# Two blocks of a language model on one core: the second token tile of x is loaded through ScalarE's queue, ahead of the norm rows and the first constants

## The chip, the core and the metric

The kernel runs on one core of a Trainium2 chip. The metric is the device time of one execution in microseconds (us), from the first instruction to the last. It is taken several times, and the median is compared.

## What is computed

The input x is 256 tokens by 1024 features, all in float32. Two layers of a first block and one layer of a second block are applied to it. Each layer of the first block is a feed-forward stage, a mixer (attention in layer 0, a state-space mixer in layer 1) and another feed-forward stage. The change touches only the very beginning, which feeds the first feed-forward stage:

```python
def rms_norm(x, g):
    xf = x.astype(jnp.float32)
    y = xf * lax.rsqrt(jnp.mean(xf * xf, axis=-1, keepdims=True) + EPS)
    return (y * g.astype(jnp.float32)).astype(x.dtype)

def swiglu(x, w_gate, w_up, w_down):
    return (jax.nn.silu(x @ w_gate) * (x @ w_up)) @ w_down

# first thing in the block
x = x + 0.5 * swiglu(rms_norm(x, ffn1_norm[i]), ffn1_w_gate[i], ffn1_w_up[i], ffn1_w_down[i])
```

## The kernel before, in words

**Tiling.** x lives in SBUF as two token tiles of 128 tokens (TT = 2), each 128 partitions by 1024 values, 512 KB. Weights come from HBM in units of 1 MB (128 x 2048 values) into three slots of `raw`. Each unit is split into a high part (`w_hi`, a copy in float32r made by ScalarE, ACT) and a low part (`w_lo`, the rest, made by VectorE, DVE). TensorE (PE) multiplies high by high, low by high and high by low. The activations are split the same way, into `hT_hi` and `hT_lo`. Programs of the engines are written out by hand and are joined by semaphores alone: an engine does its instructions in order and stops at the first one whose semaphore has not come.

**The order at the start**, which is all that the change is about:

- SyncE (SP) issues the loads of x (`start_sp`, L898 to L900), one DMA for each token tile, both counted on the semaphore `x_in`. Behind them on the same queue stand the first weights: the first unit in four DMAs of 256 KB (`first_unit`, L659 to L664: gate and up for k = 0 and 1, counted on `first_in`, then gate and up for k = 2 and 3, counted on `landed_0`), then two DMAs of 512 KB for each of units 1 and 2 (`load_unit`, L373). These eight weight loads need no wait, since the three slots are empty. The next unit waits for a slot.
- ACT issues two small loads (`start_act_loads`, L908 to L910): 64 KB of the first constants, which hold the identity matrix, and 8 KB of norm rows of ffn1 (16 x 128 values, in L905). Both are counted on `const1_in`. Then ACT waits for both (L1003), uses the identity once (L1004), which also loads its table, and waits for `cols`.
- PE (`start_pe`, L980 to L987) first does 10 matmuls on zeros (`keep_busy`, L978). Then it waits for `const1_in` to reach 32, that is, for identity and norm rows both, and transposes the norm rows (L985). Then it waits for `x_in` to reach 32, both token tiles, and transposes x in 16 pieces (L631). Four more matmuls on zeros follow, and then the first feed-forward stage, whose three kinds of products are L705, L712 and L718.
- DVE zeroes the operand of the matmuls on zeros (L1034), waits for the transposed norm rows and copies them to `cols` (L1037). ACT needs `cols` for its first `hT_hi` tile.
- After that ACT goes in this order (`start_act`): `hT_hi` tiles 0 and 1 (L553), wait for `first_in`, quarters 0 and 1 of the first unit's `w_hi` (L1009), `hT_hi` tiles 2 and 3, wait for `landed_0`, quarters 2 and 3, `hT_hi` tiles 4 and 5, unit 1's `w_hi` (L390), and so on. PE's first products need a quarter of `w_hi` and a tile of `hT_hi` each.

Of the kernel before, what the change touches and what calls it, by code (L numbers as in the profile page):

```python
# [24 lines left out]
P = 128  # L25
SEQ = 256
TT = SEQ // P
# [117 lines left out]
def build(nc, w, out):  # L145
    with ExitStack() as ctx:
        sems = {}

        def sem(name):
            if name not in sems:  # L150
                sems[name] = ctx.enter_context(nc.semaphore(name))
            return sems[name]
# [21 lines left out]
        def keep(name, shape, dt=F32):  # L174
            t, top[0] = at(top[0], name, shape, dt)
            return t
# [11 lines left out]
        x = keep("x", [P, TT, D])  # L188
# [707 lines left out]


        def start_sp(sp):  # L898
            for t in range(TT):
                sp.dma_start(x[:, t, :], w["x"][0, t * P:(t + 1) * P, :]).then_inc(sem("x_in"), 16)  # L900

        def load_rows(engine, names, landed):
            for name in names:
                a, n = ROWS[name]
                engine.dma_start(rows_in[a:a + n, :], w[name].rearrange("l (r c) -> (l r) c", c=P))\  # L905
                      .then_inc(sem(landed), 16)

        def start_act_loads(act):  # L908
            act.dma_start(const1[:, 0:P], w["first_constants"][:, 0:P]).then_inc(sem("const1_in"), 16)
            load_rows(act, ["ffn1_norm"], "const1_in")  # L910

        def start_pool(pool):
            pool.memset(neg_half[:, :], -0.5).then_inc(sem("neg_half"), 1)
# [87 lines left out]
        def start_act(act):  # L1001
            start_act_loads(act)
            act.wait_ge(sem("const1_in"), 32)  # L1003
            act.activation(table_use[:, :], ident[:, 0:1], ACT.Copy)  # L1004
            act.wait_ge(sem("cols"), 1)

            def first_hi(k):
                cs = slice(k * UNIT // 4, (k + 1) * UNIT // 4)
                act.activation(w_hi[:, 0, cs], raw[:, 0, cs], ACT.Copy).then_inc(sem("first_hi" if k < 3 else "hi_ready"), 1)  # L1009

            hT_hi_tiles(act, 0, ("ffn1_norm", 0), (0, 1))
            act.wait_ge(sem("first_in"), 16 * PARTS)
            first_hi(0)
            first_hi(1)
            hT_hi_tiles(act, 0, ("ffn1_norm", 0), (2, 3))
            act.wait_ge(sem("landed_0"), 16 * PARTS)
            first_hi(2)
            first_hi(3)
            hT_hi_tiles(act, 0, ("ffn1_norm", 0), (4, 5))
            split_hi(act, 1)  # L1020
            hT_hi_tiles(act, 0, ("ffn1_norm", 0), (6, 7))
            squares(act, 0)
            split_hi(act, 2)
# [1592 lines left out]
        @block.sync  # L2616
        def _(sp):
            start_sp(sp)
            ffn_sp(sp, "ffn1_0", FFN1, 0)
            attn_sp(sp)  # L2620
            ffn_sp(sp, "ffn2_0", FFN2, 0)
            ffn_sp(sp, "ffn1_1", FFN1, 1)
            ssm_sp(sp)
            ffn_sp(sp, "ffn2_1", FFN2, 1)
            second_sp(sp)
# [83 lines left out]
```

## Time and profile before

| | |
|---|---|
| median of 3 runs | 1322.38 us (1322.37 to 1322.51) |
| the profiled execution, its own time | 1323.11 us |
| its span, first instruction to last | 1321.3 us |
| PE busy | 1308.9 us, 99% of the span |
| DVE busy | 1079.3 us, 82% |
| ACT busy | 713.4 us, 54% |
| HBM read | 252.12 MB, 192 GB/s over the span |

The profiled execution took 0.73 us more than the median of the three runs. The rows below speak of that execution. "Busy" is time in which an instruction of the engine runs, "issue to landing" of a DMA ends when its semaphore is complete. SPq and ACTq are the queues on which SP and ACT issue DMAs. In the lists of DMA traffic, q1 is what SP issues and q10 what ACT issues, and a packet is one contiguous run of bytes on one of the 16 DMA engines, or the 4 bytes that count a semaphore up. A row of one token tile of x is a packet of 4 KB, a row of the identity matrix 512 bytes, a row of a first gate or up load 1 KB.

### The profile page before, as it was taken

The numbers are of one execution on the slowest core, as the hardware profiler recorded it, in microseconds if no ns is written. First come the engines' busy times: TensorE is split into PE (matmuls) and PEld (weight loads), VectorE is DVE, ScalarE is ACT, GpSimd is POOL, SyncE is SP. The second block draws the span as 40 slices with busy tenths as digits, with TensorE's granted clock in tenths as the row PEclk, the third lists the DMA queues.
The fourth block names the chain that finished last, engine by engine and source line by source line (L and its number), as shares of the span: only waits on it lengthen the run. The fifth ranks groups of instructions, "written<-read, shape, count | busy, mean of one in ns | idle before, by whom it ended". The sixth has DMA issues, their size and how long they took to land.

```text
span 1321.3 us, 20183 instructions
## 1 busy us (share of the span) xinstructions
PE 1308.9 (99%) x7751; PEld 1106.1 (84%) x7751; DVE 1079.3 (82%) x1592; ACT 713.4 (54%) x840; POOL 210.1 (16%) x193
## 2 busy tenths in 40 slices
PE   9999999999999999999999999999999999999998
PEld 7888888888888888888899988788888888888886
DVE  6977788868999789998786999769777767878587
ACT  6444455665444454444465688854444466558553
POOL 2400001102000010000000035300000011664940
PEclk9999999999999999999999999999999999999999
DMA  8655555528577754776544565475655554654541
GB/s 274 223 191 190 190 178 205 190 80 305 193 262 265 243 183 149 266 234 223 180 160 160 179 210 181 138 254 166 209 195 197 194 173 160 201 172 141 175 150 57
DMA packets 158445, 254.29 MB, mean 192 GB/s; under 512 B 8800, under 2 KB 99248, under 8 KB 156704
## 3 DMA queue, kind: packets, MB, share of 16 engines
q1 hardware_dynamic: 155136, 232.68, 52.1%
q0 software_dynamic: 2576, 18.45, 4.0%
q10 hardware_dynamic: 656, 2.11, 0.5%
q8 instruction: 52, 0.85, 0.2%
q14 instruction: 25, 0.20, 0.0%
HBM read 252.12 MB, written 1.08 MB: 192 GB/s over the span
## 4 chain that ended last, share of the span: by engine, by line
PE 96%; ACT 1%; DVE 1%; POOL 1%; issue 1%; DMA 0%; SPq 0%; POOLq 0%; DVEq 0%; ACTq 0%
PE psum L712 12%; PE psum L718 12%; PE psum L705 12%; PE psum L737 5%; PE psum L736 5%; PE psum L735 5%; PE psum L2003 4%; PE psum L2005 4%; PE psum L2004 4%; PE psum L438 2%; PE psum L439 2%; PE psum L445 2%; PE psum L473 2%; PE psum L481 2%; PE psum L475 2%; PE psum L504 2%
## 5 line engine op out<-in xcount | busy, mean ns | idle before, releaser
L390 ACT ACTIVATE w_hi<-raw 128x2048 fp32r<-128x2048 f32 (+1 forms) x220 | 419.8, 1910 | 316.4 <-PE psum L718 121.5
L402 DVE TENSOR_TENSOR w_lo<-raw,w_hi 128x2048 fp32r<-128x2048 f32 x219 | 507.3, 2337 | 100.2 <-ACT w_hi L390 98.7
L839 DVE STREAM_TRANSPOSE hidT<-hid 32x128 f32<-32x128 f32 x704 | 213.1, 303 | 22.1
L705 PE MATMUL psum<-w_hi,hT 128*128 128x512 f32 x704 | 174.6, 390 | 0.1
L718 PE MATMUL psum<-w_lo,hT 128*128 128x512 f32 x704 | 173.9, 389 | 0.0
L712 PE MATMUL psum<-w_hi,hT 128*128 128x512 f32 x704 | 173.9, 389 | 0.0
L712 PEld LDWEIGHTS psum<-w_hi,hT 128*128 128x128 f32 x704 | 132.2, 188 | 27.4
L718 PEld LDWEIGHTS psum<-w_lo,hT 128*128 128x128 f32 x704 | 132.2, 188 | 27.4
L705 PEld LDWEIGHTS psum<-w_hi,hT 128*128 128x128 f32 x704 | 131.9, 188 | 27.8 <-ACT w_hi L1009 0.8
L786 ACT ACTIVATE silu_g<-psum,rstd 128x256 f32<-128x256 f32 x88 | 36.9, 471 | 113.2 <-PE psum L718 107.6
L2003 PE MATMUL psum<-w_hi,hT 128*128 128x512 f32 x224 | 88.8, 397 | 0.0
L2005 PE MATMUL psum<-w_hi,hT 128*128 128x512 f32 x224 | 87.4, 390 | 0.0
L2004 PE MATMUL psum<-w_lo,hT 128*128 128x512 f32 x224 | 87.3, 390 | 0.0
L473 PE MATMUL psum<-hT,w_hi 128*128 128x256 f32 x256 | 62.6, 285 | 0.0
L737 PE MATMUL psum<-w_hi,odd_hidT_lo 128*128 128x512 f32 x160 | 62.3, 389 | 0.0
L735 PE MATMUL psum<-w_hi,hidT_hi 128*128 128x512 f32 x160 | 62.3, 389 | 0.0
L736 PE MATMUL psum<-w_lo,hidT_hi 128*128 128x512 f32 x160 | 62.3, 389 | 0.0
L735 PE MATMUL psum<-w_hi,odd_hidT_hi 128*128 128x512 f32 x160 | 62.3, 389 | 0.0
L737 PE MATMUL psum<-w_hi,hidT_lo 128*128 128x512 f32 x160 | 62.3, 389 | 0.0
L736 PE MATMUL psum<-w_lo,odd_hidT_hi 128*128 128x512 f32 x160 | 62.3, 389 | 0.0
L475 PE MATMUL psum<-hT,w_lo 128*128 128x256 f32 x256 | 62.1, 283 | 0.0
L830 DVE TENSOR_TENSOR hid<-psum,silu_g 128x512 f32<-128x512 f32 x44 | 30.3, 689 | 36.7 <-ACT silu_g L786 36.7
(407 smaller groups left out, 2186.1 us busy)
## 6 DMA issues: line engine op xcount, KB each, us to landing
raw<-in_ffn_w_down SPq DMA_DIRECT2D x88, 512.0 KB, 4.9
raw<-in_ffn_w_gate SPq DMA_DIRECT2D x87, 512.0 KB, 3.8
raw<-in_ffn_w_up SPq DMA_DIRECT2D x87, 512.0 KB, 5.1
raw<-in_w_in SPq DMA_DIRECT2D x72, 512.0 KB, 4.5
raw<-in_ssm_w_in SPq DMA_DIRECT2D x48, 512.0 KB, 4.6
raw<-in_attn_w_qkv SPq DMA_DIRECT2D x24, 512.0 KB, 4.6
ada_in<-in_w_ada POOLq DMA_DIRECT2D x8, 1536.0 KB, 7.2
raw<-in_ssm_w_out SPq DMA_DIRECT2D x16, 512.0 KB, 4.3
```

Source lines behind the costliest of these rows:

```text
L390: act.activation(to, src, ACT.Copy).then_inc(sem("hi_ready"), 1)
L402: dve.tensor_tensor(to, src, hi.bitcast(F32), ALU.subtract).then_inc(sem("lo_ready"), 1)
L705: pe.matmul(psum[:, banks[t], :], hT_hi[:, k, t * P:(t + 1) * P], hi[:, kk, :], start=k == 0, stop=False)
L712: pe.matmul(psum[:, banks[t], :], hT_lo[:, k, t * P:(t + 1) * P], hi[:, kk, :], start=False, stop=False)
L718: m = pe.matmul(psum[:, banks[t], :], hT_hi[:, k, t * P:(t + 1) * P], lo[:, kk, :], start=False, stop=k == KD - 1)
L735: pe.matmul(to, a, hi[:, k, cs], start=start and k == 0, stop=False)
L736: pe.matmul(to, a, lo[:, k, cs], start=False, stop=False)
L737: m = pe.matmul(to, b, hi[:, k, cs], start=False, stop=False)
L839: dve.transpose(to[:, :, :, 32 * a:32 * (a + 1)], src[:, :, :, 32 * b:32 * (b + 1)])\
L2003: pe.matmul(to, a, hi[:, kk, :], start=k == 0, stop=False)
L2004: pe.matmul(to, a, lo[:, kk, :], start=False, stop=False)
L2005: m = pe.matmul(to, b, hi[:, kk, :], start=False, stop=k == KD - 1)
```

## The change

```diff
         def start_sp(sp):
-            for t in range(TT):
-                sp.dma_start(x[:, t, :], w["x"][0, t * P:(t + 1) * P, :]).then_inc(sem("x_in"), 16)
+            sp.dma_start(x[:, 0, :], w["x"][0, 0:P, :]).then_inc(sem("x_in"), 16)
...
         def start_act_loads(act):
+            act.dma_start(x[:, 1, :], w["x"][0, P:2 * P, :]).then_inc(sem("x_in"), 16)
+            load_rows(act, ["ffn1_norm"], "const1_in")
             act.dma_start(const1[:, 0:P], w["first_constants"][:, 0:P]).then_inc(sem("const1_in"), 16)
-            load_rows(act, ["ffn1_norm"], "const1_in")
```

SP loads only the first token tile of x, and its weight loads move up by one place. ACT loads the second token tile first, then the norm rows, then the identity matrix. No wait is added or removed, and no byte more or less is loaded. Two places of the program differ, both queues of loads.

ACT's instructions at the start of the program (L908 is the load of the second token tile, L904 that of the norm rows, L910 that of the identity; L1004 is the first instruction that needs them):

```order
@@ -1,5 +1,6 @@
 L2642 UNCONDITIONAL_BRANCH
-L909 DMA const_58<-in_first_constants 128x128
-L905 DMA rows_in<-in_ffn_norm 16x128
+L908 DMA x<-in_x 128x1024
+L904 DMA rows_in<-in_ffn_norm 16x128
+L910 DMA const_58<-in_first_constants 128x128
 L1004 ACT_TABLE_LOAD
```

The identity goes from first to third place, and a load eight times its size now stands ahead of it.

SP's instructions at the start of the program (L663 issues the first unit's quarters of 256 KB):

```order
@@ -1,4 +1,4 @@
 L2616 UNCONDITIONAL_BRANCH
-L900 DMA x<-in_x 128x1024 x2
+L899 DMA x<-in_x 128x1024
 L663 DMA raw<-in_ffn_w_gate 128x2x256
 L663 DMA raw<-in_ffn_w_up 128x2x256
```

One load less stands ahead of the first weights. The instructions of PE, DVE and GpSimd are the same in both, and their order too.

## Rows read from the trace of the kernel before

**Rows 1.** The page: busy time of each engine, and the chain that ended last

```profile
PE 1308.9 (99%) x7751; PEld 1106.1 (84%) x7751; DVE 1079.3 (82%) x1592; ACT 713.4 (54%) x840; POOL 210.1 (16%) x193
...
PE 96%; ACT 1%; DVE 1%; POOL 1%; issue 1%; DMA 0%; SPq 0%; POOLq 0%; DVEq 0%; ACTq 0%
```

**Rows 2.** Chain that ended last, first 12.5 us: start, duration, what

```profile
1.65 0.43 SPq L663
...
2.12 6.19 DMA raw<-in_ffn_w_up
...
8.33 1.16 ACT w_hi L1009 x2
9.49 0.72 ACT hT L553 x2
10.21 0.53 ACT w_hi L1009
...
10.78 1.25 PE psum L705 x4
```

**Rows 3.** Timeline, first 9 us: start, duration, what, idle time before it

```profile
0.74 0.86 SPq L900 DMA_DIRECT2D x<-in_x  x2
0.74 0.41 ACTq L909 DMA_DIRECT2D const<-in_first_constants  x1
...
1.18 0.45 ACTq L905 DMA_DIRECT2D rows_in<-in_ffn_norm  x1
...
1.45 4.41 PE L978 MATMUL psum<-hidT_lo 128*128 128x512 f32 x10 [1.45 <-DVE hidT_lo L1034]
...
6.16 0.20 ACT L1004 ACTIVATE half_rstd_and_use<-const 128x1 f32<-128x1 f32 x1 [3.21 <-DMA rows_in<-in_ffn_norm]
...
6.18 0.23 PE L985 MATMUL psum<-const,rows_in 16*128 16x16 f32 x1 [0.31 <-DMA rows_in<-in_ffn_norm]
...
6.86 1.97 PE L631 MATMUL psum<-const,x 128*128 128x128 f32 x16 [0.45 <-DMA x<-in_x]
7.40 0.84 ACT L553 ACTIVATE hT<-psum,cols 128x256 fp32r<-128x256 f32 x2 [1.04 <-PE psum L631]
```

**Rows 4.** The instructions of tile x: time from issue to landing of its two loads

```profile
DMA to landing us min/median/max: 4.7/5.2/5.6
```

**Rows 5.** Stretches of half a microsecond: busy time of each engine, PEclk, DMA share, GB/s

```profile
2.50:3.00 0.50, 0.50 (x3) 0.40 (x2) 0.00 (x0) 0.44 (x1) 0.00 (x0) 1.00 0.34 90
3.00:3.50 0.50, 0.50 (x3) 0.40 (x2) 0.00 (x0) 0.00 (x0) 0.00 (x0) 1.00 0.66 116
...
4.50:5.00 0.50, 0.50 (x2) 0.34 (x2) 0.00 (x0) 0.00 (x0) 0.00 (x0) 1.00 1.07 420
6.00:6.50 0.50, 0.23 (x1) 0.13 (x1) 0.06 (x1) 0.20 (x1) 0.00 (x0) 1.00 1.07 381
```

**Rows 6.** DMA traffic from 0 to 4.0 us, by queue: packets, MB, share of 16 engines

```profile
q1 hardware_dynamic: 88, 0.36, 33.7%
q10 hardware_dynamic: 58, 0.03, 9.0%
```

**Rows 7.** DMA traffic by queue from 4.25 to 4.5 us

```profile
q1 hardware_dynamic: 28, 0.09, 88.8%
q10 hardware_dynamic: 30, 0.01, 17.6%
```

**Rows 8.** DMA traffic by queue from 4.75 to 5.0 us

```profile
q1 hardware_dynamic: 26, 0.10, 99.6%
q10 hardware_dynamic: 16, 0.00, 7.7%
```

**Rows 9.** DMA traffic by queue from 6.25 to 6.5 us

```profile
q1 hardware_dynamic: 97, 0.09, 104.2%
```

**Rows 10.** Timeline, 5 to 15 us: start, duration, what, idle time before it

```profile
6.83 1.81 SPq L373 DMA_DIRECT2D raw<-in_ffn_w_up  x1
...
9.59 2.44 PE L705 MATMUL psum<-w_hi,hT 128*128 128x512 f32 x8
...
11.30 0.30 PEld L705 LDWEIGHTS psum<-w_hi,hT 128*128 128x128 f32 x2 [0.22 <-ACT w_hi L1009]
...
12.85 1.92 ACT L390 ACTIVATE w_hi<-raw 128x2048 fp32r<-128x2048 f32 x1 [0.88 <-DMA raw<-in_ffn_w_up]
```

**Rows 11.** Chain that ended last, 12 to 40 us: start, duration, what

```profile
15.70 1.81 PE psum L705 x8
17.51 1.81 PE psum L712 x8
```

## The prediction

> **What bounds the kernel now.** I began with the page: PE is busy for 99% of the span and makes 96% of the chain that ended last; DMA is 0% of it, rounded [rows 1]. So loads can matter only where PE has nothing to do yet. The change touches just such a place. Its whole field is the start, so I went on to the chain of the first 12.5 us, from its end backwards [rows 2]. PE's products L705 at 10.78 wait for the third quarter of w_hi, which ACT ends at 10.74. That stands in ACT's order behind two hT tiles and two earlier quarters, which began at 8.33. The trace puts this start down to the load of the first up weights, issued at 2.12 and landed 6.19 later, at 8.31. But the timeline shows a second cause that was nearly as late: ACT's first two hT tiles ran from 7.40 for 0.84, to 8.24 [rows 3]. The gap is 0.09 us. So **two chains meet at 8.3**: the first weights (8.31), and x to transposes to hT (8.24). Whichever ends later starts w_hi.
>
> I then followed the second chain back [rows 3]. ACT's hT began 0.54 after PE's first transpose of x at 6.86. That transpose waited for x: the second load of x is the one issued at about 1.18 (two issues in 0.86 from 0.74), and the longer landing time of 5.6 [rows 4] puts it at 6.8. Before it PE had transposed the norm rows at 6.18, released by identity and norm rows together, so const1_in was complete at about 6.15. That leaves const1_in a **slack of some 0.6 us** ahead of x before it delays anything. The change spends this slack: it puts 512 KB ahead of what const1_in counts.
>
> Last I looked at how DMA engines share their time. Between 2.5 and 3.5 us they are busy for only 0.34 and 0.66 of the time, though all of x has been issued; from 4.5 on they are full at 380 to 420 GB/s [rows 5]. In the full phase the two queues take turns packet by packet: 28 packets of q1 go with 30 of q10 in 0.25 us [rows 7]. One packet of 4 KB takes 0.25 x 16 x 99.6% / 26 = 0.15 us of an engine, one of 512 bytes 0.25 x 16 x 7.7% / 16 = 0.02 us [rows 8], one of 1 KB 0.25 x 16 x 104.2% / 97 = 0.04 us [rows 9].
>
> **The change part by part.**
>
> *Issuing.* SP issues one load less ahead of the weights, 0.43 us; ACT one more. ACT's table load and L1004 come later by that, but ACT sat idle 3.21 us before L1004 [rows 3], which hides it. On SP the later loads gain nothing from it: the last of them took 1.81 us merely to issue [rows 10], since the queues are full and the bytes set the pace. All bytes that have to land before 8.31 (both tiles of x, constants, first gate and up) are the same as before. Cost 0, gain in the second term below.
>
> *x lands earlier.* Ahead of the last row of x, an engine used to carry 8 packets of the identity and one of norm rows, 9 x 0.02 = 0.2 us. These now come behind it. That gives 6.8 - 0.2 = 6.6. There may be more, from the half-empty start. Up to 4.0 us q10 carried 58 packets with 0.03 MB, and q1 88 with 0.36 MB [rows 6]. If q10's packets are as many when they are rows of x, they carry 58 x 4 KB = 0.24 MB, that is 0.21 MB more by 4.0, and at the 0.10 MB in 0.25 us of the full phase [rows 8] this is 0.5 us. If the start is slow because of the bytes, it is 0. No row shows which engine waits for what there, and the last engine counts, so I take the middle, 0.25, and keep 0 and 0.5 as ends. x_in is complete at about **6.35** (6.1 to 6.6).
>
> *const1_in lands later.* Behind the last row of x, an engine has one packet of norm rows and 8 of the identity, with their two counting packets. Taking turns with SP's queue, where rows of 1 KB now stand, this takes 9 to 11 x (0.02 + 0.04) = 0.6 us. If nothing took turns it would be 0.2. So const1_in is complete at 6.35 + 0.6 = **6.95** (6.55 to 7.2), 0.8 later than before, and **it, not x, is what PE waits for last**.
>
> *What hangs on it.* PE transposes the norm rows 0.03 after, and the transposes of x follow one matmul later; these are 0.11 apart (16 in 1.97 with the tail of the last [rows 3]). So the first starts at 6.95 + 0.03 + 0.11 = 7.09, against 6.86: +0.23. Queued behind it on PE are all other transposes, the four matmuls on zeros and L705. DVE's copy to cols takes its turn beside the transposes, as before. ACT's hT pair ends at 8.24 + 0.23 = 8.47. The first weights landed at 8.31 at the latest, so hT now sets the start of w_hi: 8.33 + 0.23 - 0.09 = 8.47 or so, **+0.14**, rounded +0.15. From there ACT's work is the same, and PE's waits for w_hi at 10.78 and 11.30 [rows 2, 10] move along.
>
> *Is the delay taken up later?* ACT has an idle 0.88 before unit 1's w_hi at 12.85 [rows 10], so ACT recovers. PE doesn't: after 11.3 it runs product after product, 8 in 1.81 us, with no gap [rows 11], and for the rest of the program it is the 96% of the chain. So the +0.15 stays to the end, and so would a gain. Weights are no danger: unit 1 is split at 12.85 + 1.92 = 14.77, PE comes to it at 15.70.
>
> **The sum**: 1321.3 + 0.15 = 1321.45 of span in a profiled execution whose own time would be 1323.11 + 0.15 = 1323.26; on the median of the runs shown, 1322.38 + 0.15 = **1322.5 us**. Bounds of the unknown terms: const1_in at 7.2 with no gain at the start gives 7.34 - 6.86 - 0.09 = +0.4. The start's full gain of 0.5 with a batch of small packets gives const1_in at 6.3 and transposes at 6.44, -0.42 - 0.09 = -0.5, and weights 0.5 earlier allow it. So the bounds are -0.5 and +0.4.
>
> A rule speaks against the change's first part. The packets of the two queues lie on the same 16 engines, whose share reaches 1.07 [rows 5]. The Trainium skill, "DMA: Bandwidth & Descriptors", section "Issuing engines are not separate DMA queues", says that issuing from several engines saves only the sequencer's issue time. By it the start's fill would be at most the 0.43 us of one issue, and the sum would hardly differ.
>
> **The rivals.**
>
> 1. *Coarse turns, slower.* The place is PE's wait for const1_in. If an engine carries a whole load of one queue (16 rows of 1 KB and a count, 17 x 0.04 = 0.7 us) before it turns to the other, the identity waits for a whole gate load: x at 6.35, plus 0.7 + 0.2 = 7.25, or 7.95 if two gate or up loads get in between. Transposes start at 7.4 to 8.1, and the kernel is 0.45 to 1.15 slower: 1322.8 to 1323.5. It decides from the moment const1_in passes 6.8. Against it: q10's 30 small packets among q1's 28 large ones in a quarter microsecond [rows 7]. The Trainium skill, the same page, section "Queues, rings and completion order", has engines drain a whole packet of some 9 to 17 descriptors of one ring before they switch; the trace's mix speaks for finer turns.
> 2. *The start fills up, faster.* The start is slow for want of rows, and the second queue supplies them: x at 6.1 or before, const1_in by 6.6, so both chains end early. It gives -0.1 to -0.5: 1321.9 to 1322.3. For it: engines 0.34 busy at 2.5 us [rows 5]. Against: const1_in is last in line.
> 3. *TensorE's clock falls, slower.* The pause between the first matmuls on zeros, which end at 5.86, and the transposes grows from 1.0 to 1.2 us or more, with only L985 in it. The first ten matmuls took 4.41 us [rows 3], 0.44 each, against 1.81 / 8 = 0.23 later [rows 11], about the ratio of the two levels, 1.2 and 2.4 GHz, though the granted clock reads 1.00 in both [rows 5]. If the low pace came back for another 4.4 us, the cost would be 4.4 x (1 - 0.23 / 0.44) = 2.1 us, in all +2.3: 1324.7. Over 0.2% it would come only if the low pace lasted 5.5 us or more. Against it: a pause of 1.0 us leaves no slow matmul now.
> 4. *Nothing moves.* If const1_in and x both come before 6.95 and weights still land at 8.31, w_hi starts where it did: 1322.4.
>
> **How the numbers follow.** My forecast, up to +0.4, has 0.4. Rival 4, nothing moves, has 0.1. Coarse turns have 0.15, a filled start 0.28, the clock 0.04, something else 0.03. The predicted time is 1322.5. The range of 8 in 10 reaches from the filled start's -0.5 to the lower half of coarse turns, with 0.1 for the scatter of the runs at either end: 1321.8 to 1323.3. A measurement of this kernel can tell about 0.2%, 2.6 us, from no change. All cases but a long-lasting fall of the clock lie within it: same 0.97, slower 0.02, faster 0.01.
>
> **What would show it.** In the changed profile the transpose of the norm rows should be released at 6.9 to 7.2, not 6.18, with transposes of x 0.1 behind it and no wait for x of their own; the longest landing of x should be 5.4 to 5.9 us from an issue at 0.74; ACT's w_hi should follow directly on hT, without a wait for the load, at about 8.5; L705's last wait should end at 11.4. The forecast is wrong if transposes of x still wait for x, if w_hi starts before 8.3, or if L705 shows a pace of 0.44.

## The result, and the profile after

The changed kernel takes 1325.07 us in the median of 20 runs (1323.38 to 1326.69); the kernel before took 1322.48 (1322.34 to 1322.84) beside it. The ratio is 1.0019, with a 95% interval of 1.0012 to 1.0025: 2.6 us slower, against +0.15 in the forecast, and above the range that ended at 1323.3. Two things stand out at once. The change costs more than any bound I gave for the loads. And the runs, which lay within 0.5 us before, now scatter over 3.3 us: 7 of the 20 lie at 1323.4 to 1324.2, 13 at 1324.8 to 1326.7.

The profiled execution of the changed kernel is one of its fastest, 1323.70 us with a span of 1321.9. Its chain of the first 14 us (start, duration, what) answers to [rows 2]:

```profile
0.74 0.41 ACTq L908
...
1.18 0.45 ACTq L904
...
1.66 5.87 DMA const<-in_first_constants
...
7.58 0.23 PE psum L985
7.81 1.90 PE psum L631 x16
9.70 0.93 PE psum L978 x4
10.63 2.09 PE psum L705 x8
```

The load of the identity, issued at 1.66 and complete at 7.53, is now the longest piece of the chain. Behind it come PE's transposes, the matmuls on zeros and the first products, each directly on the one before. In [rows 2] it was the first up load.

The timeline of the same kernel (start, duration, what, idle time before it), against [rows 3]:

```profile
0.74 0.41 ACTq L908 DMA_DIRECT2D x<-in_x  x1
...
1.45 4.64 PE L978 MATMUL psum<-hidT_lo 128*128 128x512 f32 x10 [1.45 <-DVE hidT_lo L1034]
...
7.58 0.23 PE L985 MATMUL psum<-const,rows_in 16*128 16x16 f32 x1 [1.49 <-DMA const<-in_first_constants]
...
7.74 1.97 PE L631 MATMUL psum<-const,x 128*128 128x128 f32 x16
...
8.28 0.84 ACT L553 ACTIVATE hT<-psum,cols 128x256 fp32r<-128x256 f32 x2 [0.52 <-PE psum L631]
...
9.01 1.15 ACT L1009 ACTIVATE w_hi<-raw 128x512 fp32r<-128x512 f32 x2
```

PE waits 1.49 us for the identity with nothing to do, from 6.09 to 7.58. The transposes of x wait for nothing of their own, and w_hi follows hT without a gap for the load. x itself came early: the instructions of tile x give, for its two loads, both issued at 0.74,

```profile
DMA to landing us min/median/max: 4.7/4.9/5.1
```

so x was complete at 5.84, 1.7 us before the identity. In stretches of half a microsecond, the DMA engines are fuller at the start than in [rows 5] (0.34 and 0.66, at 90 and 116 GB/s). Whether the change does this, a second profile of the kernel before answers below.

```profile
2.50:3.00 0.50, 0.50 (x3) 0.40 (x2) 0.00 (x0) 0.50 (x1) 0.00 (x0) 1.00 0.66 221
3.00:3.50 0.50, 0.50 (x3) 0.41 (x2) 0.00 (x0) 0.44 (x1) 0.00 (x0) 1.00 1.03 418
```

### The profile page after: what moved, and what is told of

It reads as the page before. It is cut to its first block, busy times and chain, and to the rows that moved or that the text cites. A ratio compares the mean times of both kernels' runs of the same rounds, so it can differ in the third digit from the quotient of the medians.

```text
span 1321.9 us, 20183 instructions
## 1 busy us (share of the span) xinstructions
PE 1308.9 (99%) x7751; PEld 1105.4 (84%) x7751; DVE 1079.7 (82%) x1592; ACT 713.3 (54%) x840; POOL 208.6 (16%) x193
## 4 chain that ended last, share of the span: by engine, by line
PE 96%; DVE 1%; ACT 1%; POOL 1%; issue 1%; DMA 0%; POOLq 0%; ACTq 0%; DVEq 0%
PE psum L705 12%; PE psum L712 12%; PE psum L718 12%; PE psum L735 5%; PE psum L736 5%; PE psum L737 5%; PE psum L2003 4%; PE psum L2004 4%; PE psum L2005 4%; PE psum L438 2%; PE psum L439 2%; PE psum L445 2%; PE psum L473 2%; PE psum L481 2%; PE psum L475 2%; PE psum L504 2%
## 5 line engine op out<-in xcount | busy, mean ns | idle before, releaser
L705 PE MATMUL psum<-w_hi,hT 128*128 128x512 f32 x704 | 174.5, 390 | 0.0
L705 PEld LDWEIGHTS psum<-w_hi,hT 128*128 128x128 f32 x704 | 131.8, 188 | 27.7 <-ACT w_hi L1009 0.6
```

The costliest lines, as they stand in the source:

```text
L705: pe.matmul(psum[:, banks[t], :], hT_hi[:, k, t * P:(t + 1) * P], hi[:, kk, :], start=k == 0, stop=False)
```

## The experiments

I had two questions: what makes the scatter and the slower two thirds of the runs, and why the identity comes so late. For the first, one theory was TensorE's clock, the other that the new order of loads costs something later. For the second, one theory was that an engine carries a whole load of one queue before it turns to the other (coarse turns), the other that it alternates packet by packet, as I had assumed.

### The changed kernel again

No edit.

> The changed kernel once more, unchanged, beside the others on the same chip. Its 20 timed runs lay between 1323.4 and 1326.7 us, those of before between 1322.3 and 1322.8; the profiled one was among its fastest (1323.7, span 1321.9). The clock theory (PE's pause of 1.5 us between the first matmuls on zeros and the transposes lets TensorE's clock rise late or fall back in a part of the executions) expects the same scatter of about 3 us, and, if the profile falls on one of the slower runs, matmuls of L631, L978 or L705 at the slow pace of 0.43 us for 512 columns. The order theory (the loads come in another order, which costs later, at the weights) expects no slow matmuls, but waits for w_hi, w_lo or DMA that are longer than in the first profile.

Measured: 1324.87 us in the median of 11 runs (1323.50 to 1326.56), before 1322.52 beside it, ratio 1.0015 (1.0006 to 1.0024). This time the profile fell on a slower run, 1325.76, span 1324.0. Its timeline:

```profile
1.45 4.19 PE L978 MATMUL psum<-hidT_lo 128*128 128x512 f32 x10 [1.45 <-DVE hidT_lo L1034]
...
7.94 0.23 PE L985 MATMUL psum<-const,rows_in 16*128 16x16 f32 x1 [2.30 <-DMA const<-in_first_constants]
...
8.10 3.43 PE L631 MATMUL psum<-const,x 128*128 128x128 f32 x16
```

Stretches of the same execution; the third number from the end is the granted clock:

```profile
7.50:8.10 0.60, 0.16 (x2) 0.14 (x2) 0.00 (x0) 0.19 (x1) 0.00 (x0) 1.00 1.08 348
8.50:11.00 2.50, 2.50 (x14) 2.50 (x13) 1.76 (x4) 2.36 (x6) 0.00 (x0) 0.50 1.11 351
12.00:14.00 2.00, 2.00 (x10) 1.63 (x9) 2.00 (x5) 2.00 (x4) 0.00 (x0) 1.00 1.10 348
```

**The granted clock reads 0.50, that is 1.2 GHz, just when PE has something to do again**, after a pause of 2.3 us. It had reached 2.4 GHz only shortly before the pause: from the second to the ninth the matmuls on zeros start 0.43 us apart, the pace of the lower level, although the granted clock reads 1.00 there. The tenth starts only 0.22 behind the ninth, at 5.25:

```profile
5.25 0.39 PE L978 MATMUL psum<-hidT_lo 128*128 128x512 f32 x1
```

The 16 transposes of x take 3.43 us here and 1.97 in the first profile. Behind them the matmuls on zeros end later, and L705 begins at 12.49, without a wait for w_hi. The five waits of PE that the profile lists from 13 us on are those of the first profile, none longer by more than 0.1 us. The order theory falls.

How much that costs can be read off, since PE has no gap afterwards: in the first profile the transposes start at 7.74 and the span is 1321.9; here they start at 8.10, 0.36 later, and the span is 1324.0, 2.1 more. So 2.1 - 0.36 = **1.7 us are the clock's** in this execution.

Not every one of the longer times need be of this kind. The mean granted clock is 0.997 in five of the 13 longer runs of the result, but 0.999 in the three longest (1326.65 to 1326.69). Profiles further down show a slow pace while the granted clock reads 1.00; that these three are of that sort isn't shown.

### The pause covered

```diff
-BUSY_BEFORE_X, BUSY_AFTER_X = 10, 4
+BUSY_BEFORE_X, BUSY_AFTER_X = 14, 4
```

> The changed kernel with 14 matmuls on zeros in place of 10, so that PE's pause is covered up to about 7 us or to 7.5. Clock theory: the scatter goes away and what is left is the delay that the profile showed, +0.6 to +0.7: 1323.0 to 1323.2 with all runs within 0.5 us. Order theory: no difference, 1325 with a scatter of 3 us.

Measured: 1323.96 us, and the 11 runs lie between 1323.80 and 1324.58, ratio 1.0011 (1.0002 to 1.0020). The scatter is down from 3.1 to 0.8 us, and no run is above 1324.6, where 6 of 11 were without the extra matmuls. In its timeline PE still waits for the identity, for 0.58 us, but the transposes run at the full pace:

```profile
7.89 0.23 PE L985 MATMUL psum<-const,rows_in 16*128 16x16 f32 x1 [0.58 <-DMA const<-in_first_constants]
...
8.05 1.97 PE L631 MATMUL psum<-const,x 128*128 128x128 f32 x16
```

So of the whole 2.35 us in this comparison (1324.87 - 1322.52), 0.9 go away when the pause is covered. The other 1.44 stay, and they are twice what I expected. That needs its own explanation (below, the kernel before again).

### The pause alone

```diff
-BUSY_BEFORE_X, BUSY_AFTER_X = 10, 4
+BUSY_BEFORE_X, BUSY_AFTER_X = 7, 4
```

This is an edit of the kernel before; the loads are untouched.

> The kernel before with 7 matmuls on zeros in place of 10: loads untouched, but PE pauses from about 4.8 us to 6.2 and, with one small transpose in between, to 6.9. Clock theory: the scatter of about 3 us appears here too, and the median rises by 1 to 3 us (1323.5 to 1325.5). Order theory: 1322.4, as before.

Measured: 1323.47 us (1322.27 to 1323.83), +0.95 against before. Three of 11 runs are as fast as before (1322.3 to 1322.5), the other eight 0.6 to 1.3 slower. The ratio, 1.0005, has an interval of 0.9996 to 1.0014, so the medians alone don't settle it; the two groups of runs and the profile do:

```profile
6.16 3.34 PE L631 MATMUL psum<-const,x 128*128 128x128 f32 x16 [0.36 <-DMA x<-in_x]
```

The transposes run at the slow pace with no change to any load. It isn't a fall of the clock this time. All seven matmuls on zeros ran at the slow pace too and the granted clock reads 1.00 throughout, so the rise came late. The direction is the clock theory's, the size is smaller than it said: the slow pace is over by 9.3 us here, when the four matmuls on zeros take 1.15 us, and part of it lies under ACT's work on hT and w_hi, on which PE would have waited anyway.

### The two small loads first on ACT's queue

```diff
-            act.dma_start(x[:, 1, :], w["x"][0, P:2 * P, :]).then_inc(sem("x_in"), 16)
+            act.dma_start(const1[:, 0:P], w["first_constants"][:, 0:P]).then_inc(sem("const1_in"), 16)
             load_rows(act, ["ffn1_norm"], "const1_in")
-            act.dma_start(const1[:, 0:P], w["first_constants"][:, 0:P]).then_inc(sem("const1_in"), 16)
+            act.dma_start(x[:, 1, :], w["x"][0, P:2 * P, :]).then_inc(sem("x_in"), 16)
```

> The changed kernel with ACT's three loads in the order identity, norm rows, second token tile: the identity and rows first, as before, x on two queues. Both theories expect const1_in at 6.2 or sooner and x at 5.9 to 6.4, so PE's transposes start at 6.0 to 6.5, 0.4 to 0.9 ahead of before. The first weights then decide: they land at 8.3 if the bytes set the pace (nothing gained, 1322.3 to 1322.4), at 7.6 to 8.0 if the start fills up as in the changed kernel's profile (-0.3 to -0.7, 1321.7 to 1322.1). Clock theory: no scatter, since the pause is no longer than before.

Measured: 1326.14 us (1324.87 to 1328.11), ratio 1.0029 (1.0019 to 1.0040). What both theories expected did not come:

```profile
8.69 2.81 PE L631 MATMUL psum<-const,x 128*128 128x128 f32 x16 [2.39 <-DMA x<-in_x]
```

This row of its timeline shows PE idle for 2.39 us, for x. Now the second token tile, issued third on ACT's queue at 1.66, is the late one; it was complete at 8.66, 7.0 us after its issue. Whatever stands third on ACT's queue comes very late, large or small. In second place it doesn't: in the first profile of the change the norm rows landed at 6.3, 0.4 behind x and some 1.2 ahead of the identity. This made coarse turns worth a test.

### First weights in smaller loads, and in larger ones

Smaller: eight loads of 128 KB in place of four of 256 KB.

```diff
-                for k in (0, 2):
+                for k in range(4):
                     for side, src in enumerate((gate, up)):
-                        sp.dma_start(dst[:, k:k + 2, FC * side:FC * (side + 1)], src[:, k:k + 2, 0:FC])\
-                          .then_inc(sem("landed_0" if k else "first_in"), 16)
+                        sp.dma_start(dst[:, k:k + 1, FC * side:FC * (side + 1)], src[:, k:k + 1, 0:FC])\
+                          .then_inc(sem(("first_in", "first_in", "third_in", "landed_0")[k]), 16)
```

ACT's waits follow: `first_in` at 64, and `third_in` besides `landed_0`.

> The changed kernel with its first weight unit in 8 loads of 128 KB in place of 4 of 256 KB. Turn theory (an engine carries a whole load of one queue, then one of the other: x0 and x1, then gate, norm rows, up, identity): the two weight loads ahead of the identity are half as long on an engine, 8 rows instead of 16, 2 x 0.37 us less in all, so const1_in is complete at 6.8 to 7.2 instead of 7.5 to 7.9. Fine turns (packet by packet) with a late supply of the identity's rows: const1_in stays at 7.5 to 7.9. The kernel's time isn't forecast closely, since the weights are issued later.

Larger: two loads of 512 KB.

```diff
-                for k in (0, 2):
-                    for side, src in enumerate((gate, up)):
-                        sp.dma_start(dst[:, k:k + 2, FC * side:FC * (side + 1)], src[:, k:k + 2, 0:FC])\
-                          .then_inc(sem("landed_0" if k else "first_in"), 16)
+                for side, src in enumerate((gate, up)):
+                    sp.dma_start(dst[:, 0:4, FC * side:FC * (side + 1)], src[:, 0:4, 0:FC])\
+                      .then_inc(sem("landed_0"), 16)
```

> The opposite of e5: the changed kernel with its first weight unit in 2 loads of 512 KB in place of 4 of 256 KB. Turn theory: a gate and an up load with 32 rows for each engine stand ahead of the identity in place of 16, 2 x 0.7 us more, const1_in complete at 8.8 to 9.3, and the time 1325 to 1327, with scatter from the clock. Fine turns: const1_in stays at 7.5 to 7.9.

Neither edit touches ACT's queue. The first use of the identity, on PE, in the timelines of the smaller and then of the larger loads:

```profile
7.15 0.23 PE L985 MATMUL psum<-const,rows_in 16*128 16x16 f32 x1 [1.06 <-DMA const<-in_first_constants]
```

```profile
8.28 0.23 PE L984 MATMUL psum<-const,rows_in 16*128 16x16 f32 x1 [2.20 <-DMA const<-in_first_constants]
```

The identity comes at 7.1 with the small loads, at 7.5 to 7.9 with the loads of the change (three profiles), and at 8.26 with the large ones. So it moves with the length of the loads on the **other** queue, which fine turns don't allow. Each end is one profile, and the three in the middle already lie 0.4 apart, but the times of the runs go the same way. The times are, for the small loads, 1323.33 us (1323.10 to 1324.71), ratio 1.0010 (1.0000 to 1.0019), and for the large ones 1326.08 (1325.03 to 1327.26), ratio 1.0029 (1.0019 to 1.0039). For the small loads the coarse turns gave the right number, 6.8 to 7.2. For the large ones they said 8.8 to 9.3, a step of 1.4, and only 0.4 to 0.7 came. So the turns look coarse, but "always one whole load" is too simple.

### Which queue carries what

The identity on SP's queue, behind the first tile:

```diff
             sp.dma_start(x[:, 0, :], w["x"][0, 0:P, :]).then_inc(sem("x_in"), 16)
+            sp.dma_start(const1[:, 0:P], w["first_constants"][:, 0:P]).then_inc(sem("const1_in"), 16)
...
-            act.dma_start(const1[:, 0:P], w["first_constants"][:, 0:P]).then_inc(sem("const1_in"), 16)
```

> The changed kernel with the identity moved to SP's queue, right behind the first token tile; ACT keeps second tile and norm rows. Turn theory: order on an engine x0, x1, identity, norm rows, gate, up, so both x_in and const1_in are complete at 5.9 to 6.3, the transposes start by 6.4, and no long pause of PE is left: 1322.2 to 1322.7, hardly any scatter. Fine turns: the identity lands by 6.0 too, the norm rows at 6.3: nearly the same. If the delay of const1_in isn't what costs, the time stays at 1324 to 1325.

Measured: 1322.59 us (1322.35 to 1324.57), ratio 1.0002 (0.9993 to 1.0011). Nine of 11 runs lie at 1322.35 to 1322.79, two at 1324.5. So one line, the place of the identity, gives back nearly the whole loss. The profile caught one of the two:

```profile
6.71 0.28 PE L985 MATMUL psum<-const,rows_in 16*128 16x16 f32 x1 [0.63 <-DMA rows_in<-in_ffn_norm]
```

The identity landed at 6.0, but the norm rows, second on ACT's queue, only at 6.7, against 5.9 to 6.3 expected. PE was idle for only 0.63 us, less than in the profiles of the change, and yet the transposes took 3.67 us. All ten matmuls on zeros had run at the slow pace, and from 7 to 10 us the granted clock reads 1.00. So this is again a late rise and not a fall, and a long pause isn't needed for it. Hardly any scatter was expected, and two runs of 11 lay 2 us above the others.

Identity, then second tile on ACT; norm rows on SP:

```diff
             sp.dma_start(x[:, 0, :], w["x"][0, 0:P, :]).then_inc(sem("x_in"), 16)
+            load_rows(sp, ["ffn1_norm"], "const1_in")
...
-            act.dma_start(x[:, 1, :], w["x"][0, P:2 * P, :]).then_inc(sem("x_in"), 16)
-            load_rows(act, ["ffn1_norm"], "const1_in")
             act.dma_start(const1[:, 0:P], w["first_constants"][:, 0:P]).then_inc(sem("const1_in"), 16)
+            act.dma_start(x[:, 1, :], w["x"][0, P:2 * P, :]).then_inc(sem("x_in"), 16)
```

> As e4, but the norm rows go to SP's queue, behind the first token tile: ACT loads identity, then the second token tile. Turn theory: x0, identity, norm rows, x1, gate: the second tile has only small loads and x0 ahead of it, so it lands at 6.0 to 6.8, against 8.7 in e4, where a gate and an up load got their turns before it. Fine turns with the pace set by bytes: in e4 and here alike, since the same bytes stand ahead in its own queue (8.0 or later). Time by the turn theory 1322.3 to 1322.8, otherwise 1325 or more.

Measured: 1322.52 us (1322.30 to 1323.16), ratio 1.0001 (0.9992 to 1.0010), the second tile complete by 6.3. Against the kernel with the small loads first, only the 8 KB of norm rows changed queues. With them the second tile moved from third to second place, and SP's weights are issued 0.46 us later; the tile lands 2.4 us sooner. The traffic by queue shows one queue at a standstill. From 4.5 to 4.75 us:

```profile
q10 hardware_dynamic: 28, 0.10, 104.8%
q1 hardware_dynamic: 5, 0.00, 2.0%
```

and from 4.75 to 5.0:

```profile
q10 hardware_dynamic: 25, 0.10, 103.2%
```

SP had issued gate and up at 1.64 and 2.10, yet q1 moves almost nothing in this half microsecond, while q10 carries 50 rows of the tile. From 5.0 us on rows of both move side by side. That gate's rows were ready by 4.5 us isn't shown; in the kernel with the small loads first, where gate was issued at 1.18, 54 packets of q1 moved only 0.07 MB between 3.75 and 4.0 us, so such rows were among them.

Identity and norm rows both on SP's queue, ACT with the second tile alone:

```diff
             sp.dma_start(x[:, 0, :], w["x"][0, 0:P, :]).then_inc(sem("x_in"), 16)
+            sp.dma_start(const1[:, 0:P], w["first_constants"][:, 0:P]).then_inc(sem("const1_in"), 16)
+            load_rows(sp, ["ffn1_norm"], "const1_in")
```

> The changed kernel with identity and norm rows on SP's queue behind the first tile, ACT with the second tile alone. Turn theory: x0, x1, identity and norm rows, gate: both semaphores at 5.9 to 6.4. The first weights are issued one place later than in e6, which costs nothing where the bytes set the pace: 1322.2 to 1322.7.

Measured: 1322.69 us in the median (1322.48 to 1323.17, and one run of 1631.93, with a mean granted clock of 0.753 where the others have 0.998 to 0.999), ratio 1.0002 (0.9993 to 1.0011), as expected; const1_in complete at 6.3.

### A version meant to beat both

```diff
         def start_pool(pool):
+            pool.dma_start(const1[:, 0:P], w["first_constants"][:, 0:P]).then_inc(sem("const1_in"), 16)
+            load_rows(pool, ["ffn1_norm"], "const1_in")
```

with the same two lines taken from ACT.

> A version meant to beat both: the second token tile on ACT's queue as in the changed kernel, identity and norm rows on GpSimd's, a third queue with turns of its own. Turn theory: they stand behind at most one load of each of the other queues, so const1_in is complete at 4.8 to 6.0 and x at 5.8 to 6.1; then the first weights (7.5 to 7.7) decide: 1322.2 to 1322.5, no pause of PE longer than before, so no scatter. If GpSimd's queue is late or slow in the start, const1_in comes after 6.5 and the time is 1322.8 or more.

Measured: 1325.27 us (1323.83 to 1326.58), ratio 1.0022 (1.0013 to 1.0031). It failed by its stated condition: GpSimd issued at 1.23 and 1.99, half a microsecond and more behind the others, and const1_in was complete only at 7.46. The later issue isn't all of it: the norm rows also took 5.5 us to land, so a third queue wasn't served ahead of the long loads as the turn theory had it. The pause of PE was 1.81 us, and the granted clock fell to 0.50 at about 8.5 us. No version tried beats the kernel before.

### The kernel before, again

No edit.

> The kernel before, once more, for a second profile. The profile that the prediction was made from took 1323.11 us, 0.6 to 0.7 more than the median of its timed runs; in two later kernels that load x in nearly the same way, x was complete at 6.1 to 6.3 us, not 6.8. If that first profile caught an unusually slow start of the DMA engines, this one has a span of 1320.5 to 1321.0, x complete at 6.0 to 6.4 and the first w_hi at 7.6 to 7.9. If the later kernels differ by what they changed, it reads as the first one: 1321.3, 6.8 and 8.3.

Measured: 1322.49 us (1322.07 to 1322.89), and in the profile a span of 1320.5, 0.8 less than in the one the prediction used. Its chain of the first 12.5 us, to be laid beside [rows 2]:

```profile
2.12 5.39 DMA raw<-in_ffn_w_up
...
7.53 1.15 ACT w_hi L1009 x2
```

and its transposes of x:

```profile
6.09 1.97 PE L631 MATMUL psum<-const,x 128*128 128x128 f32 x16
```

Up to the first products the loads make the difference: they land 0.7 to 0.8 us sooner. x was complete at about 6.1 (issued at 1.18, longest landing 4.9), const1_in at 5.8. The stretches of [rows 5] read here:

```profile
2.50:3.00 0.50, 0.50 (x3) 0.41 (x2) 0.00 (x0) 0.45 (x1) 0.00 (x0) 1.00 0.69 255
3.00:3.50 0.50, 0.50 (x3) 0.41 (x2) 0.00 (x0) 0.00 (x0) 0.00 (x0) 1.00 1.00 387
```

So the DMA engines fill as early with all of x on one queue as they did in the changed kernel (0.66 and 1.03). The fuller start was not the change's doing. The first profile had caught a slow start of the DMA engines. The sign was there: its own time was 0.73 above the median.

### Does the cover free the version with the identity on SP from its runs at 1324.5?

```diff
-BUSY_BEFORE_X, BUSY_AFTER_X = 10, 4
+BUSY_BEFORE_X, BUSY_AFTER_X = 12, 4
```

> e6 (identity on SP's queue behind the first tile) with 12 matmuls on zeros in place of 10. In e6 9 of 11 runs lay at 1322.35 to 1322.8 and two at 1324.5, and the profile, one of these two, showed transposes of x at the slow pace. Clock theory: with the pause of PE covered up to 6.3 to 6.7 us the two slow ones go away: all runs at 1322.3 to 1322.9, median 1322.5. If the slow ones have another cause, about one run in five stays at 1324.5.

Measured: 1322.99 us (1322.32 to 1323.63), ratio 1.0003 (0.9994 to 1.0012). The runs at 1324.5 are gone, as the clock theory said, though two of 11 against none of 11 proves little by itself, and the median isn't 1322.5. In the profile the twelve matmuls on zeros last until after the identity has come (ACT used it at 6.37, PE only at 6.87): here the cover itself delays PE by 0.5 us.

## Why the prediction was wrong

**What bounds the start** was read rightly: two chains meet at the first w_hi, PE has no gap afterwards, and a delay there stays to the end. Transposes that start at 7.31, 7.74 and 8.05 us (small loads, change, pause covered) give spans of 1321.5, 1321.9 and 1322.2. That the change spends const1_in's slack and makes it the last wait of PE was right too.

**x lands earlier**: the time came out earlier than I took, but by luck. It was 5.84 instead of 6.35, and up to 4.0 us q10 carried 61 packets with 0.25 MB, where I had worked out 58 with 0.24 as the upper end [rows 6]. But the kernel before fills its start as well: in its second profile 0.64 MB had moved by 4.0 us, against 0.59 in the changed kernel. Against its 6.1 the change brings x in 0.2 us earlier in one profile and at 6.0 in the other. The term that I put at 0 to 0.5 for a filled start, and rival 2 with its chance of 0.28, rested on the slow start of one execution.

**const1_in lands later** is the first step that failed. I put the distance between x and const1_in at 0.6 us, by turns packet by packet, and measured is 7.53 - 5.84 = 1.7 in the first profile and about 1.9 in the second. [rows 7], 28 packets against 30, are a sum over 16 engines that are out of step with each other, and such a sum looks the same for coarse and for fine turns. A stretch in which one queue stands still, as above, speaks for coarse turns; I had none. Rival 1 gave the right time for const1_in (7.25 to 7.95, measured 7.5 to 7.9), with a chance of 0.15. Its mechanism is the one that the runs favour, in a weaker form; its price of at most 1.15 us, against 1.44, was worked out from the untypical base, the second step. The rule that I weighed there, from the Trainium skill, "DMA: Bandwidth & Descriptors", section "Queues, rings and completion order" (a whole packet of some 9 to 17 descriptors before the ring is changed), was nearer to the runs than my reading. One first load is 16 rows and a count for an engine, and the larger loads of 32 rows didn't cost in proportion. The runs agree with a limit of that sort, though none shows it by itself.

**The base was untypical** is the second: x at 6.8, the first weights at 8.31 and a slack of 0.6 us for const1_in. With a usual start the slack is 0.2 (5.8 against 6.1). I compared with one execution whose loads were 0.8 us late, so the change's fastest profile looked like +0.6 (1321.9 against 1321.3). Against a usual start (x at 6.1, w_hi at 7.53, span 1320.5) the same spans are +1.4, and +1.7 for the 1322.2 with the pause covered. In the medians it is +1.44 with the pause covered.

**The clock**, rival 3, is the third and gave the scatter. Its place and price were right: I worked out 2.1 us for a full fall, and 1.7 was measured. What failed is the argument against it, that the pause of 1.0 us in the profile leaves no slow matmul. The pause became 1.5 to 2.3 us, and the slower group holds 13 of 20 runs and 6 of 11. The difference between the pause covered and not is 0.9 us in the median. I gave this rival 0.04. The sum's limit of 5.5 us of low pace for 0.2% also left out its own +0.15; with it 5.1 us would do. Over all 14 profiles, the granted clock fell to 0.50 in the four with a pause of 1.8 us or more (1.81, 2.20, 2.30 and 2.39), and in none of the other ten, whose longest is 1.49. The late rise, seen in two of those ten, was in neither my rival nor its price.

Together: 1.44 for the order of the loads and 0.9 for the clock make the 2.35 of that comparison; in the first one, with 2.6 in all, about 1.15 is left for the clock by difference. Against the bound of 0.2% the result lies just at the edge, as the 0.97 for no change said; but the range of 1321.8 to 1323.3 was far too narrow.

**Left open.** How long exactly an engine stays with one queue: the small loads fit whole-load turns, the large ones at most half, and the second tile in third place came at 8.66. My estimate for it by whole-load turns is 7.0 to 7.7, from the 6.3 that it took in second place and one or two loads of 0.7 us. That the place behind other loads makes const1_in late is shown, by three versions that undo it; how the engines choose between the queues is argued from few profiles. Also open is why the start of the DMA engines is sometimes 0.8 us late, and what makes the clock rise late in some runs.

## What to carry to other kernels

A small load that many wait for doesn't belong behind others on a second queue: what it has to wait for are far more rows of both queues than its own bytes suggest. Ask of a longer wait not only what it costs but what it does to the clock of the engine that waits, since an engine that starts again at a low clock pays a second time. And take a second profile of the base where the one at hand took longer than its timed runs: here it hid 0.8 of the 1.4 us that the loads cost.

## What the runs showed of the hardware

- The granted clock of TensorE fell from 1.00 to 0.50 after a pause of 2.3 us with no work at all, within half a microsecond of the engine's new start, and was back at 1.00 from 12.0 us on. After pauses of 1.81, 2.20 and 2.39 us, in three other versions, it fell only 0.9 to 1.2 us behind the new start. Runs of the same program differ in time as if it happened in some and not in others.
- TensorE can run at the lower pace while the granted clock reads 1.00: in all 13 profiles with ten or more matmuls on zeros (512 columns), the second to the ninth start 0.43 us apart, and in two profiles 16 transposes took 3.34 and 3.67 us, against 1.97, with the reading at 1.00.
- Of two queues that share the 16 DMA engines, one carried 53 packets in 0.5 us, 50 of them of 4 KB, while the other, with two loads issued, moved only 5 small ones.
- The loads of x were complete at about 6.1 us in one execution and at 6.8 in another of the same program.
- The norm rows, 8 KB, issued on GpSimd's queue at 1.99 us, took 5.5 us to land. On ACT's queue they took 4.6 and 5.0 us in the two profiles of the kernel before.
